# One decoder step with a routed mixture of experts: expert products on four 32-column strips, turned by VectorE

## The chip, the cores and the metric

The kernel runs on one core of a Trainium2 chip. The metric is device time in microseconds (us), lower is better; a time is the median of several executions of the whole program. One program computes the whole step; the change touches its expert phase and the layouts of what that phase reads.

## The reference

One layer of a decoder over 2048 prompt tokens and 32 sample tokens (2080 in all), 1024 wide, in fp32. After attention and a recurrent branch comes the part that matters here:

```python
def hier_moe(x, ...):            # top-1 group of 4, then top-2 of the 8 experts in it
    gates = p_sel * softmax(top_val)            # two (token, expert) pairs per token: 4160 pairs
    return routed_experts(x, experts.reshape(-1), gates.reshape(-1), w1, w3, w2)

def expert_block(args):          # rows of one expert; w1, w3: 1024 x 512, w2: 512 x 1024, 32 experts
    xb = x_pad[toks]
    hb = silu(xb @ w1[e]) * (xb @ w3[e])
    return hb @ w2[e]
# the results, times their gates, are summed per token; then x + gate2 * ffn and a final RMSNorm
```

## The kernel before

The phases follow one another: modulation and input projection, attention for both groups, the router (with the output projection), the experts, the final sum. Each phase has one hand-written stream for each engine, ordered by semaphores only.

The router writes each token's row twice (once for each chosen expert) into DRAM scratch: `xs_d0` holds the left 512 columns, `xs_d1` the right 512, rows grouped by expert. It also counts, for each expert, how many blocks of G = 64 rows it has. `experts_of` then loops over the 32 experts, and inside over the blocks of an expert (a hardware loop with a count read from memory). On this data there are 80 blocks: 1 to 4 for an expert, 2.5 on average. `n` counts blocks over all experts.

One block, engine by engine:

- GpSimd (`gpsimd`): `load(n)` waits until TensorE has turned the block before, then brings 64 rows with two DMAs (`xs_d0` to partitions 0 to 63 of `x_in`, `xs_d1` to 64 to 127; there is one such buffer). `store(n)` waits until the copy two blocks back is in `y` and until the store before has landed, then writes 64 rows of `ys_d` with one DMA. Its DRAM side is `strips`: "r (s n) -> s r n" with two strips of 512 columns, so the outermost dimension is 2. Both use GpSimd's own DMA queue (q0).
- TensorE (`tensor`): in a block, `hidden` makes x @ [w1 | w3] in two halves of 128 hidden columns on two strips (64 tokens stand as 64 columns of the array, the output lands in partitions 0 to 63 or 64 to 127): 8 chunks of 128 inputs, 2 strips, 2 halves, 256 columns each, 32 products. `turn_hidden` turns a half of the gated values through the array (L1982), `turn(n + 1)` turns the next block's rows (4 transposes, L1968), `out` makes the product with w2: 8 products of 512 columns (L1989). In the trace each fp32 product is two matmul instructions, each with its own weight load; a transpose is one.
- ScalarE (`scalar`): two sigmoids, and the copy of the turned rows from PSUM to `xT` (L1952).
- VectorE (`vector`): two multiplications for each half, the copy of the turned values to `hT` (L2027), the copy of the result to `y` (L2035).
- SyncE (`sync`): the weights, three slots. Expert e's w1, w3 and w2 (2 MB each) are issued when the last block of expert e - 3 is done (`hold` on `y`). The DRAM side is "(c p) n -> p c n": in a partition, 8 rows of 2 KB of w1 that lie 128 rows apart. They use q1.

Two buffers of `y` let results run one block ahead of their stores. What sets the order around the change: the program order of each engine, the semaphores above, and the order of DMAs inside each of the two queues.

Of the kernel before, what the change touches and what calls it, by code (L numbers as in the profile page):

```python
# [35 lines left out]
STRIPS = 2  # L36
G = P // STRIPS
XW = D // STRIPS
# [31 lines left out]
class Kit:  # L70
# [768 lines left out]
def attention_phase(nc, io, keep, sems):  # L839
# [38 lines left out]
    with ExitStack() as stack:  # L878
        k = Kit(nc, stack)
        shared = keep["w13_0"][:, :, :, :].rearrange("p c a n -> p (c a n)")  # L880
# [535 lines left out]
def router(nc, io, keep, sems, k):  # L1416
# [59 lines left out]
    def sync(sp):  # L1476
# [19 lines left out]
        for at, name in enumerate(("w1", "w3")):  # L1496
            sp.dma_start(keep["w13_0"][:, :, at, :], io[name][0, 0].rearrange("(c p) n -> p c n", p=P)).then_inc(sems["pre"], 16)
# [11 lines left out]
    def gpsimd(pool):  # L1509
# [31 lines left out]
        pool.dma_start(io["ys_d"][0:G, :].rearrange("r (s n) -> s r n", n=XW), keep["y"][:, 0, :]).then_inc(sems["st"], 16)  # L1541
# [301 lines left out]
def experts_of(nc, io, keep, sems, k, emptied):  # L1843
# [8 lines left out]
    x_in, xT = keep["o_rs"][:, :, :].rearrange("p c n -> p (c n)"), keep["o_sq"]  # L1852
    sg, hid = k.sb("sg7", [P, 2, P]), k.sb("hid", [P, 2, P])
    hT = k.sb("hT", [P, 2, P])
    y = keep["y"]
    xb, yb = keep["banks"][5], keep["banks"][3]
    h, tb = ([keep["banks"][b] for b in pair] for pair in ((4, 6), (0, 1)))
    s = {n: k.sem(f"p7_{n}") for n in ("in", "xT", "xe", "h", "sg", "hid", "hT", "he", "y", "ye", "sp")}
# [3 lines left out]
    ident = keep["ident"]  # L1862
    src = {n: io[n][0] for n in ("w1", "w3", "w2")}
    def strips(d, row):

        return d[ds(row, G), :].rearrange("r (s n) -> s r n", n=XW)

# [16 lines left out]
    def sync(sp):  # L1884
# [3 lines left out]
        sp.dma_start(w2[0][:, :, :], src["w2"][0].rearrange("(c p) n -> p c n", p=P)).then_inc(s_w2[0], 16)  # L1888
        sp.wait_ge(sems["placed"], 1)
        sp.wait_ge(s["in"], 32)  # L1890
        for e in range(NE):
# [27 lines left out]
    def gpsimd(pool):  # L1919
        pool.nop().then_inc(s["ye"], 2)  # L1920
        pool.nop().then_inc(s["xT"], 1)
# [23 lines left out]
        hold(pool, s["st"], 16 * n + 48, s["sp"])  # L1945
        hold(pool, s["in"], 32 * n + 32, s["sp"])

    def scalar(act):
        def turned(n):

            act.wait_ge(s["xT"], n + 2)
            act.activation(xT[:, :, :], xb[:, :].rearrange("p (c n) -> p c n", n=P), ACT.Copy).then_inc(s["xe"], 1)  # L1952

        def body(n, e, b, extra):
            for half in range(2):
                act.wait_ge(s["h"], 2 * n + half + 1)
                act.activation(sg[:, half, :], h[half][:, 0:P], ACT.Sigmoid).then_inc(s["sg"], 1)  # L1957
            turned(n + 1)

        act.wait_ge(sems["placed"], 1)  # L1960
        turned(0)
        experts(act, body)

    def tensor(pe):
        def turn(n):
            pe.wait_ge(s["in"], 32 * n + 32)
            for c in range(XW // P):
                mm = pe.transpose(xb[:, c * P:c * P + P], x_in[:, c * P:c * P + P], ident[:, :])  # L1968
            mm.then_inc(s["xT"], 1)

        def hidden(i, half, chunks):

            for c in chunks:
                for q in range(STRIPS):
                    cols = slice(q * (DE // STRIPS) + half * P, q * (DE // STRIPS) + half * P + P)
                    mm = pe.matmul(h[half][q * G:q * G + G, 0:2 * P], xT[:, c % (XW // P), c // (XW // P) * G:c // (XW // P) * G + G],  # L1976
                                   w13[i][:, c, :, cols], start=(c == 0), stop=(c == KC - 1))
            return mm

        def turn_hidden(n, half):  # L1980
            pe.wait_ge(s["hid"], 2 * n + half + 1)
            pe.transpose(tb[half][:, 0:P], hid[:, half, :], ident[:, :]).then_inc(s["hT"], 1)  # L1982

        def out(i, n, half):

            pe.wait_ge(s["he"], 2 * n + half + 1)
            for q in range(STRIPS):
                for p in range(STRIPS):
                    mm = pe.matmul(yb[p * G:p * G + G, :], hT[:, half, q * G:q * G + G], w2[i][:, q * (EC // STRIPS) + half, p * XW:p * XW + XW],  # L1989
# [293 lines left out]
```

## Time and profile before

| | |
|---|---|
| median of 3 executions | 2929.57 us (2927.0 to 2935.26) |
| span of the profiled execution | 2942.9 us, 13.3 us above that median; no other time of that execution is shown |
| instructions | 45551 |
| TensorE busy | 2701.4 us, 92% of the span |
| weight loads | 1377.9 us (47%), beside the matmuls |
| VectorE, ScalarE, GpSimd busy | 46%, 33%, 16% |
| DMA | 575.74 MB, mean 196 GB/s |
| expert phase | 1852.4 to 2844.0 us of the span, 991.6 us |

Busy is the time in which an engine had at least one instruction in flight. Weight loads are counted apart, as PEld. The name of a tile is the program's first name for that memory: in the expert phase `o_rs` is the landing buffer of the rows, `o_sq` the turned rows, `w`, `oT` and `w_out` the three weight slots.

### The profile page before, as it was taken

Reading aid. Unit: us, or ns where it says so; the run is one execution under the profiler, and the core shown is the slowest. Engines: PE = TensorE matmul, PEld = TensorE weight load, DVE = VectorE, ACT = ScalarE, POOL = GpSimd, SP = SyncE. Lnnn points to the kernel's source line nnn. Section 1 sums busy time; section 2 is a strip of 40 time slices with the busy share of each in tenths; the row PEclk is TensorE's granted clock in tenths of the full one; section 3 lists DMA queues with packets and bytes.
Section 4 is the critical chain, followed back from the end, with each engine's and each line's share of the span. In section 5 each row is a group of like instructions: output and inputs, shape, how many; then the busy total and the mean of one; then the engine's idle time right before and its main releaser. Section 6 shows DMA issues by size and latency. Waiting matters only on the chain. (4 is left out here: it accounts for less than half of the span.)

```text
span 2942.9 us, 45551 instructions
## 1 busy us (share of the span) xinstructions
PE 2701.4 (92%) x15113; PEld 1377.9 (47%) x15113; DVE 1352.6 (46%) x2734; ACT 961.6 (33%) x1858; POOL 472.9 (16%) x669
## 2 busy tenths in 40 slices
PE   6999999976988898998989997799999998899978
PEld 3444444433544444554535554355545554455533
DVE  2241414143887787897867776122112221122118
ACT  2222222113777776787842221100000010000004
POOL 0101010101112111211201223111111111111123
PEclk8999999997999999999999998899999999999989
DMA  8020201146667776767763334686976679969637
GB/s 321 15 86 15 81 19 65 50 148 223 212 224 261 227 242 214 250 211 245 234 231 114 129 129 157 217 280 216 300 236 216 212 234 357 305 215 300 215 103 318
DMA packets 275921, 575.74 MB, mean 196 GB/s; under 512 B 59270, under 2 KB 75719, under 8 KB 271740
## 3 DMA queue, kind: packets, MB, share of 16 engines
q1 hardware_dynamic: 192936, 427.99, 42.1%
q0 software_dynamic: 82480, 145.43, 15.4%
q8 instruction: 89, 1.46, 0.2%
q14 instruction: 92, 0.75, 0.1%
q10 hardware_dynamic: 324, 0.10, 0.0%
HBM read 460.86 MB, written 112.29 MB: 195 GB/s over the span
## 5 line engine op out<-in xcount | busy, mean ns | idle before, releaser
L1246 DVE TENSOR_TENSOR_SCAN left<-leave,left 128x512 f32<-128x512 f32 (+3 forms) x320 | 358.6, 1121 | 138.6 <-ACT leave L1128 137.9
L435 PE MATMUL bank<-xnT,w_in 128*128 128x512 f32 x768 | 330.3, 592 | 0.0
L1989 PE MATMUL bank<-w,hT 128*64 128x512 f32 x1280 | 315.1, 614 | 0.0
L1957 ACT ACTIVATE sg<-bank 128x128 f32<-128x128 f32 x160 | 44.3, 277 | 688.0 <-PE bank L1976 688.0
L1049 POOL DMA_DIRECT2D w_out<-in_cache_v x256 | 137.4, 537 | 666.8 <-issue 663.9
L1976 PE MATMUL bank<-w,o_sq 128*64 128x256 f32 x1920 | 224.2, 387 | 9.5 <-DMA w<-in_w 6.7
L435 PEld LDWEIGHTS bank<-xnT,w_in 128*128 128x128 f32 x768 | 145.6, 190 | 181.8 <-issue 179.4
L1612 PE MATMUL bank<-w_out,w 128*128 128x512 f32 x512 | 227.7, 597 | 2.6 <-DVE w L1676 2.6
L435 PE MATMUL bank<-w_in,xnT 128*128 128x512 f32 x512 | 220.4, 592 | 0.0
L2021 DVE TENSOR_TENSOR sg<-sg,bank 128x128 f32<-128x128 f32 x160 | 46.1, 288 | 375.3 <-ACT sg L1957 375.3
L1976 PE MATMUL bank<-oT,o_sq 128*64 128x256 f32 x1856 | 212.3, 381 | 0.3 <-issue 0.3
L1297 PE MATMUL tb<-ident,take 128*128 128x128 f32 x1088 | 182.5, 285 | 29.6 <-DVE take L1152 25.9
L1128 ACT ACTIVATE leave<-zb,nbiasP 128x512 f32<-128x512 f32 (+3 forms) x320 | 204.3, 638 | 8.1 <-PE zb L1290 8.0
L1130 ACT ACTIVATE take<-zb,biasP 128x512 f32<-128x512 f32 (+3 forms) x320 | 206.9, 647 | 0.0
L1152 DVE TENSOR_TENSOR take<-take,left 128x512 f32<-128x512 f32 (+3 forms) x320 | 194.8, 609 | 15.5 <-DVE left L1246 0.5
L1284 PE MATMUL zb<-w 64*128 64x512 f32 (+3 forms) x640 | 165.5, 595 | 30.4 <-ACT take L1130 19.1
L1297 PEld LDWEIGHTS tb<-ident,take 128*128 128x128 f32 x1088 | 120.5, 143 | 148.1 <-issue 80.2
L1332 PE MATMUL tb<-ident,w_out 128*128 128x128 f32 x1024 | 161.5, 282 | 25.2 <-DMA w_out<-in_cache_k 15.8
L1976 PEld LDWEIGHTS bank<-w,o_sq 128*64 128x64 f32 x1920 | 137.6, 139 | 95.5 <-issue 32.0
L1060 ACT ACTIVATE wT<-tb 128x512 f32<-128x512 f32 (+3 forms) x240 | 131.8, 549 | 126.8 <-PE tb L1297 126.1
L1976 PEld LDWEIGHTS bank<-oT,o_sq 128*64 128x64 f32 x1856 | 131.3, 137 | 80.8 <-issue 18.8
L1932 POOL DMA_DIRECT2D ys_d<-y x82 | 70.3, 857 | 551.5 <-DMA ys_d<-y 437.5
(411 smaller groups left out, 3386.5 us busy)
## 6 DMA issues: line engine op xcount, KB each, us to landing
w<-in_w SPq DMA_DIRECT2D x54, 2048.0 KB, 23.6
w_out<-in_cache_v POOLq DMA_DIRECT2D x256, 256.0 KB, 5.1
w_out<-in_cache_k SPq DMA_DIRECT2D x256, 256.0 KB, 4.0
oT<-in_w SPq DMA_DIRECT2D x22, 2048.0 KB, 19.5
w_out<-in_w SPq DMA_DIRECT2D x20, 2048.0 KB, 18.7
ys_d<-zeros SPq DMA_DIRECT2D x32, 816.0 KB
ys_d<-y POOLq DMA_DIRECT2D x83, 256.0 KB, 10.3
o_rs<-xs_d POOLq DMA_DIRECT2D x162, 128.0 KB, 6.4
```

Of the source, the lines that this page charges most:

```text
L435: mm = pe.matmul(ps[:, :], w, m, start=(i == 0), stop=(i == len(parts) - 1))
L1049: pool.dma_start(vp[g % 2][:, j, :], cache["cache_v"][ds(number, 1)].rearrange("a p n -> (a p) n")).then_inc(s_vp[g % 2], 16)
L1128: act.activation(leave[n % 4][:, 0:cols], zb[n % 3][:, 0:cols], ACT.Sigmoid, scale=-SCALE, bias=keep["nbiasP"][:, head:head + 1]).then_inc ...
L1130: act.activation(take[n % 4][:, 0:cols], zb[n % 3][:, 0:cols], ACT.Sigmoid, scale=SCALE, bias=keep["biasP"][:, head:head + 1]).then_inc(s_ ...
L1152: dve.tensor_tensor(take[n % 4][:, 0:cols], take[n % 4][:, 0:cols], left[n % 4][:, 1:cols + 1], ALU.mult).then_inc(s_w, 1)
L1246: dve.tensor_tensor_scan(left[n % 4][:, 0:cols][:, ::-1], leave[n % 4][:, 0:cols][:, ::-1], leave[n % 4][:, 0:cols][:, ::-1], left[n % 4][ ...
L1284: mm = pe.matmul(zb[(n + par) % 3][:, 0:cols], qT[pair % 2][half, t * P:t * P + P], kT[pair % 2][half, c * GRP:c * GRP + cols], start=True ...
L1297: mm = pe.transpose(to[:, j * P:j * P + P], take[n % 4][:, j * P:j * P + P], ident[:, :])
L1332: mm = pe.transpose(to[:, i * P:i * P + P], kp[g % 2][:, i, f * P:f * P + P], ident[:, :])
L1612: mm = pe.matmul(pb[half][0:n, :], lhs, w_out[:, half, c, :], start=(c == 0), stop=(c == KC - 1))
L1976: mm = pe.matmul(h[half][q * G:q * G + G, 0:2 * P], xT[:, c % (XW // P), c // (XW // P) * G:c // (XW // P) * G + G], w13[i][:, c, :, cols] ...
L1989: mm = pe.matmul(yb[p * G:p * G + G, :], hT[:, half, q * G:q * G + G], w2[i][:, q * (EC // STRIPS) + half, p * XW:p * XW + XW], start=(hal ...
```

## The change

The block stays 64 rows, but the array is now used in 4 strips of Q = 32 columns: one block is 2 units of 32 tokens (UNITS), and the four strips of a unit are four ranges of 128 hidden columns (or of 256 output columns). `hidden(i, u)` is 8 chunks times 4 strips, 256 columns each; `out(i, u)` is 4 chunks times 4 strips, 256 columns each: 96 products for a block where there were 40.

All transposes through TensorE go. VectorE's `transpose`, which turns 32x32 squares inside their place, turns the rows (`turn_rows`, 128x256 for each unit) and the gated values (128x128 for each unit). For this the squares must find their weight rows in matching order: the weights are loaded as "(p c) n -> p c n", so that a partition holds 8 rows of w1 that follow one another in DRAM, 16 KB in one piece on both sides (`w13` becomes [P, 2, KC, DE] for that), and 4 rows of w2 likewise, 16 KB. ScalarE copies the landed rows into the order that the squares want (`landed`), and takes over the copy of the result from PSUM.

The rows land in two buffers (in `rowsP`). A load of a block is 4 DMAs of 64 partitions x 1 KB, a store 2 DMAs of 128 partitions x 1 KB. Both have `in_strips` as their DRAM side: "b (s n) -> s b n"; a load's strips there are 2, a store's 4. `load` now ends with a wait for its own landing, ahead of `store`. w1 and w3 of a slot are released after the first product of its last block, w2 after the second, and TensorE waits for w2 only ahead of `out`.

```diff
-STRIPS = 2
-G = P // STRIPS
-XW = D // STRIPS
+G = 64
+STRIPS = 4
+Q = P // STRIPS
+UNITS = G // Q
+XW = UNITS * (D // STRIPS)
...
+def in_strips(d, row, u):
+    return d[ds(row + u * Q, Q), :].rearrange("b (s n) -> s b n", n=D // STRIPS)
...
-                hold(sp, s["y"], sp.snap(done, min_val=1, max_val=MAX_BLOCKS), s["sp"])
+                freed = sp.snap(done, min_val=1, max_val=MAX_BLOCKS)
+                hold(sp, s["h1"], freed, s["sp"])
...
-                    sp.dma_start(w13[i][:, :, at, :], src[name][e].rearrange("(c p) n -> p c n", p=P)).then_inc(s_w13[i], 16)
+                    sp.dma_start(w13[i][:, at, :, :], src[name][e].rearrange("(p c) n -> p c n", p=P)).then_inc(s_w13[i], 16)
...
+            if e >= SLOTS:
+                hold(sp, s["y"], freed, s["sp"])
             if e > 0:
-                sp.dma_start(w2[i][:, :, :], src["w2"][e].rearrange("(c p) n -> p c n", p=P)).then_inc(s_w2[i], 16)
+                sp.dma_start(w2[i][:, :, :], src["w2"][e].rearrange("(p j) n -> p j n", p=P)).then_inc(s_w2[i], 16)
...
         def load(n, row):
-            hold(pool, s["xT"], n + 1, s["sp"])
-            for half in range(2):
-                pool.dma_start(x_in[64 * half:64 * half + 64, :], strips(io[f"xs_d{half}"], row)).then_inc(s["in"], 16)
+            hold(pool, s["cp"], n + 1, s["sp"])
+            for u in range(UNITS):
+                for half in range(2):
+                    pool.dma_start(x_in[64 * half:64 * half + 64, ds(n & 1, 1), u * (XW // 2):(u + 1) * (XW // 2)].rearrange("p a n -> p (a n)"),
+                                   in_strips(io[f"xs_d{half}"], row, u)).then_inc(s["in"], 16)
+            hold(pool, s["in"], 64 * n + 64, s["sp"])
...
-            hold(pool, s["st"], 16 * n + 16, s["sp"])
-            pool.dma_start(strips(io["ys_d"], n * G + G), y[:, ds(n & 1, 1), :].rearrange("p a n -> p (a n)")).then_inc(s["st"], 16)
+            hold(pool, s["st"], 32 * n + 32, s["sp"])
+            for u in range(UNITS):
+                pool.dma_start(in_strips(io["ys_d"], n * G + G, u),
+                               y[:, ds(n & 1, 1), u * (XW // 2):(u + 1) * (XW // 2)].rearrange("p a n -> p (a n)")).then_inc(s["st"], 16)
...
+        def landed(n):
+            act.wait_ge(s["in"], 64 * n + 64)
+            act.wait_ge(s["xT"], 2 * n + 1)
+            act.activation(x_turn[:, :].rearrange("p (u c a) -> p u c a", u=UNITS, c=KC),
+                           x_in[:, ds(n & 1, 1), :].rearrange("p z (u a c) -> p (z u) c a", u=UNITS, c=KC), ACT.Copy).then_inc(s["cp"], 1)
...
+        def result(n):
+            act.wait_ge(s["st"], 32 * n + 64)
+            act.wait_ge(s["y"], n + 1)
+            act.activation(y[:, ds(n & 1, 1), :].rearrange("p a n -> p (a n)"), yb[:, :], ACT.Copy).then_inc(s["ye"], 1)
         def body(n, e, b, extra):
+            landed(n + 1)
+            for u in range(UNITS):
+                gated(n, u)
+            result(n)
...
+        def hidden(i, u):
+            for c in range(KC):
                 for q in range(STRIPS):
+                    mm = pe.matmul(h[u][q * Q:q * Q + Q, 0:2 * P], xT[:, c, u, :], w13[i][:, :, c, q * P:q * P + P], start=(c == 0), stop=(c == KC - 1))
...
+        def out(i, u):
+            for j in range(EC):
+                for q in range(STRIPS):
+                    mm = pe.matmul(yb[q * Q:q * Q + Q, u * (XW // 2):(u + 1) * (XW // 2)], hT[:, u, j, :], w2[i][:, j, q * (XW // 2):(q + 1) * (XW // 2)],
+                                   start=(j == 0), stop=(j == EC - 1))
...
         def body(n, e, b, extra):
             i = e % SLOTS
+            for u in range(UNITS):
+                pe.wait_ge(s["xT"], 2 * n + u + 2)
+                hidden(i, u).then_inc(s[f"h{u}"], 1)
+            pe.wait_ge(s_w2[i], 16 * (e // SLOTS) + 16)
+            for u in range(UNITS):
+                pe.wait_ge(s["hT"], 2 * n + u + 1)
+                mm = out(i, u)
+            mm.then_inc(s["y"], 1)
...
+        def turn_rows(n, u):
+            dve.wait_ge(s["cp"], n + 3)
+            dve.transpose(xT[:, :, u, :], x_turn[:, u * (XW // 2):(u + 1) * (XW // 2)]).then_inc(s["xT"], 1)
         def body(n, e, b, extra):
+            for u in range(UNITS):
+                dve.wait_ge(s["sg"], 2 * n + u + 1)
+                dve.tensor_tensor(sg[:, u, :], sg[:, u, :], h[u][:, 0:P], ALU.mult)
+                dve.drain()
+                dve.tensor_tensor(hid[:, u, :], sg[:, u, :], h[u][:, P:2 * P], ALU.mult)
+                dve.drain()
+                dve.transpose(hT[:, u, :, :].rearrange("p j b -> p (j b)"), hid[:, u, :].rearrange("p (a j) -> p j a", j=EC)).then_inc(s["hT"], 1)
+                turn_rows(n + 1, u)
```

## Rows read from the trace of the kernel before

**Rows 1.** Engine busy time in stretches: us, (x instructions), clock, DMA share, GB/s
```profile
2287.10:2333.50 46.40, 46.40 (x346) 24.93 (x344) 9.72 (x28) 4.61 (x12) 7.60 (x13) 1.00 0.55 181
2453.50:2468.50 15.00, 12.21 (x89) 6.24 (x85) 3.12 (x8) 1.15 (x3) 1.92 (x3) 0.98 1.05 360
1852.40:2844.00 991.60, 950.35 (x6880) 504.62 (x6880) 193.58 (x559) 97.22 (x244) 153.57 (x240) 0.98 0.75 249
```

**Rows 2.** Timeline of TensorE, one block: start, us, line, shapes, x instructions
```profile
2298.70 5.78 PE L1976 MATMUL bank<-oT,o_sq 128*64 128x256 f32 x52
2304.41 0.33 PE L1982 MATMUL bank<-ident,hid 128*128 128x128 f32 x1
2308.00 0.60 PE L1968 MATMUL bank<-ident,o_rs 128*128 128x128 f32 x4
2308.54 1.94 PE L1989 MATMUL bank<-w,hT 128*64 128x512 f32 x8
2310.31 1.90 PE L1976 MATMUL bank<-oT,o_sq 128*64 128x256 f32 x16
```

**Rows 3.** Timeline of TensorE elsewhere: products on four strips of 32 columns
```profile
674.44 1.04 PE L727 MATMUL ps_mod<-ig,cT 128*32 128x512 f32 x8
675.30 1.04 PE L727 MATMUL ps_mod<-yb,cT 128*32 128x512 f32 x8
753.86 0.88 PE L1368 MATMUL tb<-kT_new,q_blk 128*32 128x4 f32 x32
```

**Rows 4.** Groups of instructions in the expert phase: busy, mean ns | idle before, releaser
```profile
L2035 DVE COPY y<-bank 128x512 f32 x79 | 54.7, 692 | 221.0 <-PE bank L1989 195.9 <-DMA ys_d<-y 25.1
L1982 PE MATMUL bank<-ident,hid 128*128 128x128 f32 x160 | 52.5, 328 | 0.0
L1952 ACT ACTIVATE o_sq<-bank 128x512 f32<-128x512 f32 x80 | 47.8, 597 | 204.8 <-PE bank L1968 204.8
L2027 DVE COPY hT<-bank 128x128 f32<-128x128 f32 x160 | 46.7, 292 | 196.3 <-PE bank L1982 196.3
L2021 DVE TENSOR_TENSOR sg<-sg,bank 128x128 f32<-128x128 f32 x160 | 46.1, 288 | 375.3 <-ACT sg L1957 375.3
```

**Rows 5.** Timeline of ScalarE and VectorE behind the last product of a second half
```profile
1954.13 1.89 PE L1989 MATMUL bank<-w,hT 128*64 128x512 f32 x8
1954.34 0.28 ACT L1957 ACTIVATE sg<-bank 128x128 f32<-128x128 f32 x1 [3.59 <-PE bank L1976]
1955.02 0.29 DVE L2023 TENSOR_TENSOR hid<-sg,bank 128x128 f32<-128x128 f32 x1
```

**Rows 6.** Timeline of GpSimd's DMA issues
```profile
1965.34 0.86 POOL L1932 DMA_DIRECT2D ys_d<-y  x1 [6.63 <-DMA ys_d<-y]
1975.84 0.86 POOL L1932 DMA_DIRECT2D ys_d<-y  x1 [5.54 <-DMA ys_d<-y]
2309.41 1.06 POOL L1926 DMA_DIRECT2D o_rs<-xs_d  x2 [5.00 <-PE bank L1968]
```

**Rows 7.** Who waited for whom in the expert phase: us, times, longest
```profile
POOL ys_d L1932 <- DMA ys_d<-y: 437.5, 64, 12.3
PE bank L1968 <- DMA o_rs<-xs_d: 29.5, 16, 4.0
```

**Rows 8.** DMA from 2209 to 2219 us, one store and two loads, little else
```profile
GB/s 0 0 0 0 0 0 0 36 4 37 19 33 16 0 0 0 33 33 0 49 49 49 66 33 66 66 33 66 33 66 66 33 66 33 66 279 229 246 147 246
DMA packets 631, 0.55 MB, mean 55 GB/s; under 512 B 493, under 2 KB 493, under 8 KB 631
q0 software_dynamic: 621, 0.53, 21.5%
ys_d<-y POOLq DMA_DIRECT2D x1, 256.0 KB, 9.0
o_rs<-xs_d POOLq DMA_DIRECT2D x2, 128.0 KB, 2.5
```

**Rows 9.** DMA from 1975.8 to 1981.6 us, a store beside the weights
```profile
DMA packets 1228, 2.11 MB, mean 364 GB/s; under 512 B 208, under 2 KB 208, under 8 KB 1227
q1 hardware_dynamic: 1027, 2.07, 100.7%
ys_d<-y POOLq DMA_DIRECT2D x1, 256.0 KB, 13.5
```

**Rows 10.** DMA from 1486 to 1495 us: rows of 16 KB into rowsP
```profile
DMA packets 169, 1.67 MB, mean 186 GB/s; under 512 B 24, under 2 KB 24, under 8 KB 73
```

More of the change, by code:

```diff
@@ L1851, in experts_of @@
     w13, w2 = [keep[f"w13_{i}"] for i in range(SLOTS)], [keep[f"w2_{i}"] for i in range(SLOTS)]
[L1852 to L1854 removed]
+    x_in = keep["rowsP"][:, 2, :].rearrange("p (a n) -> p a n", a=2)
+    x_turn = keep["o_rs"][:, :, :].rearrange("p c n -> p (c n)")
+    xT = keep["o_sq"][:, :, :].rearrange("p c n -> p (c n)").rearrange("p (c u b) -> p c u b", c=KC, u=UNITS)
+    sg, hid = k.sb("sg7", [P, UNITS, P]), k.sb("hid", [P, UNITS, P])
+    hT = k.sb("hT", [P, UNITS, EC, Q])
     y = keep["y"]
[L1856 to L1858 removed]
+    yb, h = keep["banks"][3], [keep["banks"][b] for b in (4, 6)]
+    s = {n: k.sem(f"p7_{n}") for n in ("in", "cp", "xT", "h0", "h1", "sg", "hT", "y", "ye", "sp")}
     s["st"] = sems["st"]
@@ L1944, in gpsimd @@
         store(n + 1)
-        hold(pool, s["st"], 16 * n + 48, s["sp"])
-        hold(pool, s["in"], 32 * n + 32, s["sp"])
+        hold(pool, s["st"], 32 * n + 96, s["sp"])
     def scalar(act):
-        def turned(n):
-            act.wait_ge(s["xT"], n + 2)
-            act.activation(xT[:, :, :], xb[:, :].rearrange("p (c n) -> p c n", n=P), ACT.Copy).then_inc(s["xe"], 1)
-        def body(n, e, b, extra):
[L1955 to L1958, printed above, removed]
+        def landed(n):
[3 more added lines that the diff above has]
+                           x_in[:, ds(n & 1, 1), :].rearrange("p z (u a c) -> p (z u) c a", u=UNITS, c=KC), ACT.Copy).then_inc(s["cp"], 1)
@@ new lines, in gated @@
+        def gated(n, u):
+            act.wait_ge(s[f"h{u}"], n + 1)
+            act.activation(sg[:, u, :], h[u][:, 0:P], ACT.Sigmoid).then_inc(s["sg"], 1)
+        def result(n):
+            act.wait_ge(s["st"], 32 * n + 64)
+            act.wait_ge(s["y"], n + 1)
+            act.activation(y[:, ds(n & 1, 1), :].rearrange("p a n -> p (a n)"), yb[:, :], ACT.Copy).then_inc(s["ye"], 1)
+        def body(n, e, b, extra):
+            landed(n + 1)
+            for u in range(UNITS):
+                gated(n, u)
+            result(n)
@@ L1960, in scalar @@
+        act.nop().then_inc(s["xT"], 1)
         act.wait_ge(sems["placed"], 1)
-        turned(0)
+        landed(0)
         experts(act, body)
     def tensor(pe):
[L1965 to L1973, printed above, removed]
+        def hidden(i, u):
+            for c in range(KC):
@@ L1984, in out @@
[L1984 to L1989, printed above, removed]
-                                   start=(half == 0 and q == 0), stop=(half == 1 and q == STRIPS - 1))
+                    mm = pe.matmul(h[u][q * Q:q * Q + Q, 0:2 * P], xT[:, c, u, :], w13[i][:, :, c, q * P:q * P + P], start=(c == 0), stop=(c == KC - 1))
@@ L1994, in body @@
             i = e % SLOTS
-            pe.wait_ge(s["xe"], n + 1)
-            hidden(i, 0, range(KC)).then_inc(s["h"], 1)
-            hidden(i, 1, range(5))
-            turn_hidden(n, 0)
-            hidden(i, 1, range(5, KC)).then_inc(s["h"], 1)
-            out(i, n, 0)
-            turn_hidden(n, 1)
-            turn(n + 1)
-            out(i, n, 1).then_inc(s["y"], 1)
+            for u in range(UNITS):
[6 more added lines that the diff above has]
+            mm.then_inc(s["y"], 1)
         def before(e):
@@ L2010, in before @@
                 pe.wait_ge(s_w13[i], 32 * (e // SLOTS + (1 if i else 0)))
[L2011 removed]
         pe.wait_ge(sems["placed"], 1)
[L2014 removed]
         experts(pe, body, before)
     def vector(dve):
+        def turn_rows(n, u):
+            dve.wait_ge(s["cp"], n + 3)
+            dve.transpose(xT[:, :, u, :], x_turn[:, u * (XW // 2):(u + 1) * (XW // 2)]).then_inc(s["xT"], 1)
         def body(n, e, b, extra):
[L2019 to L2021 removed]
+            for u in range(UNITS):
+                dve.wait_ge(s["sg"], 2 * n + u + 1)
+                dve.tensor_tensor(sg[:, u, :], sg[:, u, :], h[u][:, 0:P], ALU.mult)
                 dve.drain()
[L2023 to L2036 removed]
+                dve.tensor_tensor(hid[:, u, :], sg[:, u, :], h[u][:, P:2 * P], ALU.mult)
+                dve.drain()
+                dve.transpose(hT[:, u, :, :].rearrange("p j b -> p (j b)"), hid[:, u, :].rearrange("p (a j) -> p j a", j=EC)).then_inc(s["hT"], 1)
+                turn_rows(n + 1, u)
+        for u in range(UNITS):
+            turn_rows(0, u)
         experts(dve, body)
```

46 lines of the change are left out of this document (10 added, 36 removed).

## The prediction

> **What bounds the kernel now.** I read the stretches of the expert phase first, as nothing else in the program changes its work. The phase lasts 991.6 us, TensorE is busy in 950.35 of them at clock 0.98 [rows 1]. Then one block on TensorE's timeline: from one block's first product (2298.70) to the next one's (2310.31) are 11.61 us, with no idle time in an expert of four blocks (46.40 busy of 46.40) [rows 1, 2]. The 80 blocks (160 L1982, two for each block [rows 4]) at 11.61 would take 929 us, so 63 us go elsewhere: experts of one block, which wait for 6.3 MB of weights (15.0 us for one block, DMA share 1.05 [rows 1]), the first expert, and 29.5 us in which TensorE waits for rows [rows 7]. So TensorE bounds it, but something stands close behind: GpSimd's stores wait 437.5 us in all for the store before to land [rows 7]. Stores issued at 1965.34 and 1975.84 are 10.5 us apart, with 5.54 us of waiting on the landing [rows 6]. A chain of transfers with a period of 10.5 to 14 us (9.0 to 13.5 for the landing [rows 8, 9]) lies under a product chain of 11.6 us. The reader is to see both before pricing a faster TensorE.
>
> **Products: 96 for 40.** The new block has 64 + 32 products, 192 matmul instructions of 256 columns. On four strips the trace has 512 columns: 8 instructions start at 674.44 and the next 8 at 675.30, 0.43 us for four abreast [rows 3]. Half the columns: 0.215 us for four, 48 x 0.215 = 10.3 us for a block. The same columns on two strips also make 10.3 (64 instructions of 256 columns and 16 of 512, two abreast), so the strips bring nothing by themselves. That 32-column instructions can follow one another fast enough is seen where they have 4 columns: 32 in 0.88 us, 0.028 each, against the 0.054 wanted [rows 3]. What goes is the rest, 11.61 - 10.3 = 1.3 us a block: two turns of gated values, four of rows, and the changes of shape around them [rows 2]. 80 x 1.3 = 104 us if nothing else binds.
>
> The Trainium skill (TensorE: Matmul & The Clock Gate, "The mechanism" of packing) says that a weight load overlaps products in flight only when they stand in different row groups, and here all four strips share all rows; by that, 192 loads would queue up. At 0.11 us or more each that page's rule would put over 20 us on a block; the eight instructions in 0.86 us say otherwise.
>
> **The turned values.** In the old trace the sigmoid of the second half starts 0.21 us after the next product's start (1954.34 against 1954.13), and its second multiplication ends at 1955.31, 1.18 us after it [rows 5]. A VectorE transpose isn't in the trace. Nearest is the copy of the same 128x128 shape, 0.29 us; the 128x512 copy at 0.69 is the upper bound, and below 0.29 would gain nothing because TensorE is busy [rows 4]. With 0.29 and 0.1 for the handover they are there at 1.6 us; the first unit's `out` (32 instructions at 0.054) covers 1.7. So nothing, at most 0.3 x 80 = 24 us.
>
> **ScalarE and VectorE.** ScalarE gets two 128x512 copies (0.60 each by the nearest [rows 4], up to double for the strided read) and two sigmoids of 0.28 [rows 5]: 1.8 to 3 us of 10.3. VectorE: four multiplications, two 128x128 and two 128x256 transposes, 2.6 to 4.5 us. Both wait in program order, but `landed(n + 1)` stands ahead of the sigmoids: rows that land late hold up the block in hand, once the two buffers are used up. All of this hides unless the rows are late, and that is the question.
>
> **The transfers.** A store now is 256 KB in two strips. In a quiet stretch a store and two loads (0.53 MB) leave 621 packets, 493 of them below 512 B, and through most of it only 33 to 66 GB/s flow [rows 8]. With the weights 16 engines move 364 GB/s, 23 each [rows 9]: the store flows over two engines. 0.53 MB in the 128 other packets is 4 KB each, so 64 for the store, 32 for each of two engines, and 14 x 32 = 448 of the small ones are the fillers of the other 14. It lands after 9.0 us in quiet and after 13.5 beside the weights [rows 8, 9]: 4.5 / 32 = 0.14 us for each place in the queue, about one weight packet (1027 packets of 2.07 MB, 2 KB each, 0.09 us at 23 GB/s; w2's are 4 KB, 0.18). So the two queues take turns packet by packet on each engine, fillers too.
>
> The Trainium skill (DMA: Bandwidth & Descriptors, "Queues, rings and completion order") gives the rule that the engines used are the largest number up to 16 that divides the outermost dimensions of both sides; the store's two agree with it.
>
> The new load's DRAM side has two strips outermost: two engines for each of its four DMAs, 64 KB / 2 / 4 KB = 8 places. The store's two DMAs have four strips: 128 KB / 4 / 4 KB = 8 places. Together 6 x 8 = 48 places on every engine for a block, against 32 + 2 x 2 = 36 now. And the weights become rows of 16 KB in one piece. The one transfer of such rows in the trace has 169 packets for 1.67 MB, 96 of them of 8 KB or more: they go as 16 KB packets [rows 10]. At 23 to 26 GB/s that is 0.63 to 0.7 us, four to seven times what a place costs now beside the weights.
>
> The loop on GpSimd, free of weights: four issues, 3 x 0.53 and then the landing, 2.5 [rows 6, 8], 4.1; register work between a landing and the store's issue 0.9 (1975.84 less 1965.34 less about 9.5); two stores at 0.6 to 0.86, 1.5; back to the next load 1.1 (0.8 from the release to the issue: 2308.60 to 2309.41 [rows 2, 6]). 7.6 us, well under 10.3. But `load` waits for its landing before `store` and before the next load, so the loop can't run ahead while weights stream. An expert has 6.3 MB / 16 KB / 16 = 24 weight packets on each engine, 15.6 us at 0.65. In that time at most 24 places are served, half a block: a load caught in it stands until the weights are in. What the loop still does in it is issuing, 3.6 us. So it loses 12 us for each expert. Bounds: 8 (a whole loop's own work falls into the stream) to 15.6.
>
> Sum, for an expert of 2.5 blocks: 2.5 x 7.6 + 12 = 31 us, plus 0.8: the four experts of one block take 15 us by the weights alone [rows 1], 7 over a loop. 31.8, x 32 = 1018 us, against 991.6. TensorE alone would need 2.5 x 10.3 = 25.8. The gain of 104 us is hidden behind the transfers, and 26 us are added: the span goes from 2942.9 to 2969. Its execution stood 13.3 above the median; at the median, 2929.6 + 26 = 2955. With 8 and 15.6 for 12: 890 and 1133 us, 2830 and 3070.
>
> **Rivals.** *TensorE keeps the pace.* If loads spread over 16 engines (their SBUF side has 64 partitions outermost), or weights stay in small packets, or 16 KB packets don't make the small ones wait, the loop stays under 10.3: 80 x 10.3 = 825, plus the 15 us of the first expert and 10 to 20 for experts of one block, 850 to 860, which is 2790 to 2800, and 2820 with the upper bound of the turned values; I take 2800. For it: a load that finds the queue empty lands in 2.5 us; against it: the fillers. *Half and half:* late rows only in experts of one or two blocks, 2850 to 2915. *The strips don't run abreast at 256 columns* (slower): if a group of four takes 0.43 us whatever its columns, a block takes 20.6 us and the phase 1650, over 3500; if weight loads cost 0.02 us an instruction, 14 us, 3070 and more. It decides once four instructions need over 0.24 us; the 0.028 us [rows 3] speaks against it. *The change doesn't do what it says:* weight rows that aren't joined to 16 KB give the first rival.
>
> **Numbers.** Transfers set the pace (own range 2925 to 3040): 0.50, of it 0.45 slower and 0.05 no change. TensorE keeps the pace: 0.33, faster. Half and half: 0.12, of it 0.09 faster and 0.03 no change. Strips: 0.05, slower. Faster 0.42, no change 0.08, slower 0.50; no change is within 0.3%, about what this kernel's timing can tell. The range from 2790 to 3020 leaves out some of the first rival below, and the strips and the worst transfers above.
>
> **What would show it.** Four products start within 0.03 us and the next four 0.215 later; blocks in quiet stretches take 10.3 to 10.6 us; weight packets of 16 KB, 384 for an expert; loads with fillers of their own, so more packets below 512 B than now; loads that land after over 10 us beside weights; TensorE and ScalarE waiting for the landing of rows, 150 us or more in all. Wrong would be: loads landing in 3 to 5 us throughout, or a phase below 900 us.

## The result, and the profile after

The changed kernel takes 3141.1 us (median of 6 runs, 3131.1 to 3163.3), the one before 2934.2 us beside it (6 runs): a ratio of 1.0725, 95% interval 1.0701 to 1.0750. Slower, as forecast, but by 207 us where 26 were forecast, and above the range's 3020 us.

The stretches of the profiled execution (start:end, length, busy time of TensorE's products and weight loads, VectorE, ScalarE, GpSimd, then clock, DMA share, GB/s): the expert phase, and two blocks in it that met no delay.

```profile
1846.50:3058.20 1211.70, 895.97 (x15358) 498.39 (x15360) 206.49 (x641) 184.41 (x327) 326.29 (x482) 0.87 0.60 204
2656.00:2679.00 23.00, 23.00 (x428) 13.13 (x424) 5.29 (x16) 5.24 (x9) 8.13 (x12) 0.99 0.56 174
```

The phase is 220 us longer than the 991.6 of [rows 1]; the rest of the program is 7 us shorter. TensorE has less work in it (896 us for 950) and stands idle for 316. Its timeline in the second stretch (start, us, line, x instructions):

```profile
2657.05 7.08 PE L1993 MATMUL bank<-w,o_sq 128*32 128x256 f32 x128
2663.95 3.70 PE L2000 MATMUL bank<-w,hT 128*32 128x256 f32 x64
2667.47 7.09 PE L1993 MATMUL bank<-w,o_sq 128*32 128x256 f32 x128
```

From one block's first product to the next one's are 10.42 us, against 11.61 in [rows 2] and 10.3 in the forecast. That part of the change does what it says. The groups of the phase (busy, mean ns of one, idle before, releaser), against [rows 4]:

```profile
L1935 POOL DMA_DIRECT2D rowsP<-xs_d x317 | 210.4, 672 | 81.6 <-issue 80.7 <-ACT o_rs L1965 0.6
L1965 ACT ACTIVATE o_rs<-rowsP 128x512 f32 x80 | 91.7, 1147 | 455.7 <-DMA rowsP<-xs_d 454.2 <-issue 1.3
L2037 DVE STREAM_TRANSPOSE hT<-hid 128x128 f32<-128x128 f32 x160 | 66.2, 414 | 12.6 <-issue 0.6
L2028 DVE STREAM_TRANSPOSE o_sq<-o_rs 128x256 f32<-128x256 f32 x160 | 64.4, 402 | 0.0
L1975 ACT ACTIVATE y<-bank 128x512 f32 x80 | 47.8, 597 | 387.2 <-PE bank L2000 337.4 <-DMA ys_d<-y 49.8
```

And who waited for whom (us, times, longest), against [rows 7]:

```profile
POOL ys_d L1944 <- issue: 735.2, 85, 34.1
ACT o_rs L1965 <- DMA rowsP<-xs_d: 454.2, 65, 28.0
PE bank L2000 <- DVE hT L2037: 315.2, 38, 33.4
```

The three waits are one. GpSimd stands at `load`'s wait for the landing before it may issue the store, ScalarE waits for the same rows, and TensorE for the values behind ScalarE. The timeline of all engines shows it once:

```profile
2071.73 2.65 POOL L1935 DMA_DIRECT2D rowsP<-xs_d  x4 [0.52 <-issue]
2075.01 7.09 PE L1993 MATMUL bank<-w_out,o_sq 128*32 128x256 f32 x128
2094.86 1.12 ACT L1965 ACTIVATE o_rs<-rowsP 128x512 f32 x1 [18.78 <-DMA rowsP<-xs_d]
2095.66 1.41 POOL L1944 DMA_DIRECT2D ys_d<-y  x2 [21.28 <-issue]
2096.18 0.29 DVE L2033 TENSOR_TENSOR sg<-sg,bank 128x128 f32<-128x128 f32 x1 [23.01 <-ACT sg L1970]
2097.36 1.94 PE L2000 MATMUL bank<-w,hT 128*32 128x256 f32 x16 [15.26 <-DVE hT L2037]
```

Rows issued from 2071.7 on have all landed at 2094.6. TensorE ends the block's first products at 2082.1 and waits 15.26 us: `landed(n + 1)` stands ahead of the sigmoids of block n, so rows that are late for the next block hold the one in hand. The DMA packets from 2076 to 2094 us say what was in the way (weights are q1, rows q0):

```profile
DMA packets 1003, 5.78 MB, mean 321 GB/s; under 512 B 590, under 2 KB 590, under 8 KB 671
q1 hardware_dynamic: 379, 5.42, 80.8%
q0 software_dynamic: 623, 0.34, 8.2%
```

332 packets (1003 less 671) are of 8 KB or more and 5.42 MB / 332 are 16 KB each: the weights come in packets of 16 KB. The rows' 623 packets need only 8.2% of the engines' time; most of the 23 us they aren't being moved, and the likeliest reading is that they stand in line behind the others; experiments 1 and 11 test it. The forecast had this picture and this price. What it hadn't is the other kind of block, free of weights; GpSimd's timeline of two:

```profile
2258.50 1.41 POOL L1944 DMA_DIRECT2D ys_d<-y  x2 [21.19 <-issue]
2260.43 2.65 POOL L1935 DMA_DIRECT2D rowsP<-xs_d  x4 [0.52 <-issue]
2268.28 1.41 POOL L1944 DMA_DIRECT2D ys_d<-y  x2 [5.20 <-issue]
2270.20 2.65 POOL L1935 DMA_DIRECT2D rowsP<-xs_d  x4 [0.52 <-issue]
2277.92 1.41 POOL L1944 DMA_DIRECT2D ys_d<-y  x2 [5.07 <-issue]
2280.96 2.66 POOL L1935 DMA_DIRECT2D rowsP<-xs_d  x4 [1.62 <-issue]
```

9.8 and 10.8 us from load to load, of which 5.1 to 5.2 pass between the end of the load's issues and the store. I split the loops by the trace's packets, each loop counted from the landing of one block's rows to the landing of the next: in 36 of 78 weight packets take under 0.3 us of an engine's time between the last issue of the load and its landing. These take 10.27 us on average, with 1.98 from the first issue to the last and 4.3 from there to the landing. The other 42 take 18.7, and land after 13.1. So 80 x 10.27 = 822, and the other 390 us of the phase are 12.6 for each of the 31 experts whose weights stream. That is a remainder. By the loops themselves 42 x 8.45 = 355 us are lost, 11.4 for an expert; most of what is left is the first block, ahead of whose second product TensorE waits longest, 33.4 us (the longest wait in the list above). Forecast were 7.6 for the free loop and 12 for the loss. The loss was right in size; the free loop was not.

### The profile page after: what moved, and what is told of

Its sections match the earlier page's. It is cut to its first block and busy times, and to the rows that moved or that the text cites. A ratio compares the mean times of both kernels' runs of the same rounds, so it can differ in the third digit from the quotient of the medians.

```text
span 3155.8 us, 63798 instructions
## 1 busy us (share of the span) xinstructions
PE 2642.2 (84%) x23589; PEld 1368.9 (43%) x23589; DVE 1365.3 (43%) x2816; ACT 1051.0 (33%) x1942; POOL 647.3 (21%) x914
## 5 line engine op out<-in xcount | busy, mean ns | idle before, releaser
L2000 PE MATMUL bank<-w,hT 128*32 128x256 f32 x5120 | 348.2, 431 | 315.2 <-DVE hT L2037 315.2
L2000 PEld LDWEIGHTS bank<-w,hT 128*32 128x32 f32 x5120 | 173.0, 124 | 483.3 <-DVE hT L2037 347.9
L1944 POOL DMA_DIRECT2D ys_d<-y x164 | 115.9, 712 | 810.0 <-issue 743.6
L1965 ACT ACTIVATE o_rs<-rowsP 128x512 f32 (+1 forms) x81 | 92.9, 1146 | 464.6 <-DMA rowsP<-xs_d 454.2
L1935 POOL DMA_DIRECT2D rowsP<-xs_d x324 | 215.1, 672 | 85.1 <-issue 84.2
L1993 PE MATMUL bank<-w,o_sq 128*32 128x256 f32 x3840 | 214.7, 382 | 20.0 <-DVE o_sq L2028 20.0
L1993 PE MATMUL bank<-oT,o_sq 128*32 128x256 f32 x3712 | 205.6, 379 | 0.5 <-issue 0.5
L1975 ACT ACTIVATE y<-bank 128x512 f32 x80 | 47.8, 597 | 387.2 <-PE bank L2000 337.4
## 6 DMA issues: line engine op xcount, KB each, us to landing
w<-in_w SPq DMA_DIRECT2D x54, 2048.0 KB, 15.9
```

Of the source, the lines that this page charges most:

```text
L1935: pool.dma_start(x_in[64 * half:64 * half + 64, ds(n & 1, 1), u * (XW // 2):(u + 1) * (XW // 2)].rearrange("p a n -> p (a n)"), in_strips( ...
L1993: mm = pe.matmul(h[u][q * Q:q * Q + Q, 0:2 * P], xT[:, c, u, :], w13[i][:, :, c, q * P:q * P + P], start=(c == 0), stop=(c == KC - 1))
L2000: mm = pe.matmul(yb[q * Q:q * Q + Q, u * (XW // 2):(u + 1) * (XW // 2)], hT[:, u, j, :], w2[i][:, j, q * (XW // 2):(q + 1) * (XW // 2)], s ...
```

## The experiments

All were timed beside the kernel before, whose median was between 2931 and 2937 us. "Phase" is the expert phase of the profiled execution; free loop, landing and loss are worked out as above, the loss with that run's own free loop. The changed kernel's profiled execution took 3157 us, 16 above its median, so what is saved against its phase of 1211.7 comes out about 16 us larger than in the medians.

**1. Weights in small packets.** The order of the pieces in SBUF gives 2 KB for w1 and w3, four DMAs 4 KB for w2.

```
-  w13_0 [P, 2, KC, DE];  w13[i][:, at, :, :]
+  w13_0 [P, KC, 2, DE];  w13[i][:, :, at, :]
-  sp.dma_start(w2[i][:, :, :], ...)
+  for j in range(EC): sp.dma_start(w2[i][:, j, :], ...[:, j, :])
```

> The changed kernel, but w1 and w3 land as [c, a, n] in SBUF, so that their pieces are 2 KB instead of 16 KB, and w2 comes in four DMAs of 4 KB rows; the order of the rows is the same. Theory A (GpSimd's loop of loads and stores sets the pace, and what it loses beside the weights is a 16 KB packet for each place in the queue): a place costs 0.09 to 0.18 us beside weights instead of 0.65, so of the 12.6 us lost for an expert some 5 remain; phase 80 x 10.27 + 31 x 5 = 980 us instead of 1212, time about 2910. The landing of rows beside weights falls from 13 to about 9 us. Theory B (only the loop's serial waits and issues matter, not the packet size): within 1% of 3141. Theory C (weights get slower with small packets, 16.5 us of engine time for an expert against 15.6): slightly above 3141.

Measured: 3050.8 us, ratio 1.0404 (1.0346 to 1.0461). Phase 1102. The free loop stays (10.34), the loss falls to 8.9. The direction is A's, with 90 us well short of the 231 it gave. The landing beside weights falls from 13.1 to 9.6 us, as A has it, but now 55 of 78 loads meet weights where 42 did, and the other term isn't touched.

**2. Loads on 16 engines.** Each of the four loads of a block brings one strip for all 64 rows, so that 32 pairs of rows stand outermost on the DRAM side.

```
-  for u in range(UNITS):
-      for half in range(2):
-          pool.dma_start(x_in[64 * half:64 * half + 64, ...], in_strips(io[f"xs_d{half}"], row, u))
+  for q in range(STRIPS):
+      pool.dma_start(x_in[q * Q:q * Q + Q, ...], one_strip(io[f"xs_d{q // 2}"], row, q % 2))
...
+  one_strip: d[ds(row, G), strip s].rearrange("(u b) n -> b u n", u=UNITS)
```

> The changed kernel, but each of the four load DMAs takes one strip of all 64 rows, so that 32 rows stand outermost on both sides and all 16 DMA engines share it: 1 place in the queue on each engine instead of 8, 20 places for a block instead of 48. Stores and weights as they are. Theory A: fillers and places matter. Free of weights the last load lands about 2.5 us after its issue instead of 4.3, the loop takes 8.5; beside weights a load waits behind the store's 16 places at 0.65, 10.4 us, so some 9 are still lost for an expert; phase about 2.6 x 8.5 x 31 + 9 x 31 = 960, TensorE's 10.4 a block just below; time about 2890. Theory B (serial waits, not places): the free landing stays near 4.3, time within 1% of 3141.

Measured: 3025.4 us, 1.0317 (1.0248 to 1.0385). Phase 1081. Both terms fall: the free loop to 9.44 (8.8 median), with the landing 2.4 us after the last issue for 4.3, and the loss to 10.5, with the landing beside weights at 10.5 us for 13.1. The median falls by 116 us, of A's 250. The DMA view of 8 us with one quiet load and a store, first of the changed kernel (from 2270), then of this one (from 2904.7):

```profile
DMA packets 767, 0.52 MB, mean 65 GB/s; under 512 B 643, under 2 KB 643, under 8 KB 767
rowsP<-xs_d POOLq DMA_DIRECT2D x4, 64.0 KB, 3.4
```

```profile
DMA packets 302, 0.50 MB, mean 63 GB/s; under 512 B 180, under 2 KB 180, under 8 KB 302
rowsP<-xs_d POOLq DMA_DIRECT2D x4, 64.0 KB, 3.0
```

The same bytes with 463 fewer small packets (the four loads' 4 x 14 x 8 = 448 fillers). The medians differ by 0.4 us only, because a median over four hides the last: in the quiet loops of the changed kernel the first three loads land on average 2.9 to 3.1 us after their own issue and the fourth after 4.3, here all four after 2.4 to 3.1, and the fourth is the one GpSimd waits for.

**3. The wait moved.** GpSimd issues the store before it waits for the load's landing.

```
   load(n, ...)   # without its hold
   store(n)
+  hold(pool, s["in"], 64 * n + 64, s["sp"])
```

> The changed kernel, but the wait for the rows' landing stands behind the store instead of ahead of it. Every load still lands before the next is issued. Theory A: the free loop is then issues and one landing side by side with the stores: 4 x 0.67 + 2 x 0.7 + register work 1.5 + what is left of the landing, 8 us instead of 10.27, below TensorE's 10.4, but the 12.6 us lost beside weights stay, since the next load still waits: 31 x (2.6 x 8 + 12.6) = 1035, time about 2965. Theory B (the serial wait is the whole cause): TensorE's pace, 2810. Theory C (DMA places alone, the order of waits is nothing): 3141.

Measured: 3079.1 us, 1.0500 (1.0438 to 1.0562). Phase 1136. Between A and C, nowhere near B: the landing itself is still in the loop of rows, only the store's issue isn't behind it any more. The terms behave as A has them: the free loop falls, though to 9.4 and not to 8, and the loss stays (12.4).

**4. 16 KB packets alone, in the kernel before.** Its products read the weights as they come, so the values are not the reference's.

```
-  src[name][e].rearrange("(c p) n -> p c n", p=P)
+  src[name][e].rearrange("(p c) n -> p c n", p=P)     # and w13 [P, 2, KC, DE], w2 likewise
```

> The kernel before, with one part of the change alone: weights come as 16 KB rows. The products then pair the wrong inputs with weight rows, so the output isn't the reference's; the work is the same. Theory A: a store has 32 places on each engine, an expert's weights 24 packets, so a store beside weights lands after 9 + 24 x 0.65 = 24 us instead of 13.5. The chain of stores, 10.4 us free, gets 12 to 15 us more for an expert: phase 32 x (2.5 x 10.4 + 13) = 1250, time about 3190, slower than before by 8 to 9%. Theory B (packet size doesn't matter, or larger is better): within 1% of 2934.

Measured: 3094.6 us, 1.0553 (1.0487 to 1.0619). One part of the change by itself costs 158 us. Its waits, against [rows 7]:

```profile
POOL ys_d L1932 <- DMA ys_d<-y: 506.7, 56, 26.5
PE bank L1968 <- DMA o_rs<-xs_d: 175.5, 33, 20.1
```

TensorE waits 175.5 us for rows where it waited 29.5, once for 20.1 us. The old load, on few and small packets, suffers from 16 KB neighbours as well. The weights themselves come sooner: the page of the profile has 19.9 us to landing for 2 MB into the first slot in place of 23.6.

**5. Loads and stores on 16 engines.** As 2, and the store in four strips too.

> The changed kernel with every transfer of rows cut by strips of 64 rows: four loads and four stores for a block, each of which lands on 16 engines with one place; the weights still come in packets of 16 KB. It differs from the run that cut the loads alone (3025 us) by the store: two transfers of two engines have become four of sixteen. Theory A (GpSimd's chain sets the pace; packets behind weight packets of 16 KB are what a place costs): the store's 16 places and its small packets on idle engines go, but GpSimd issues two more transfers, 2 x 0.7 us a block. Beside weights the first saves about 3 us per expert, the issues cost up to 1.4 x 80 = 112 us where nothing hides them and nothing where GpSimd waits for the landing anyway: 3000 us (2970 to 3050). Theory B (the number of issues on GpSimd is what sets the free loop): 3025 + 112 = 3137 us. Theory C (the store's small packets are what slows the loads): 2930 us.

Measured: 2997.7 us, 1.0216 (1.0189 to 1.0243). Phase 1060. A. (The store it replaces has four strips outermost in each of its two transfers, so four engines each and not two.) Two more issues a block don't cost 112 us (B): the free loop is 9.8 for 9.4. And the store's small packets aren't what held the loads (C). With 48, 20 and now 8 places for a block on an engine, rows beside weights land after 13.1, 10.5 and 8.5 us, and the loss is 12.6, 10.5 and 8.9: fewer places help, but far from in proportion.

**6. Both cuts.** 1 and 2 together.

> The changed kernel with two of its parts undone together: each load one strip of 64 rows on 16 engines, and the weights in packets of 2 and 4 KB. Alone they took the expert phase from 1211.7 us to 1081 and to 1102. Theory A (a chain on GpSimd with a free loop and a loss per expert, which the two cut in different places): free loop 9.44 us as with the loads alone, x 80 = 755; loss per expert 12.6 in the changed kernel, 10.5 with the loads cut, 3.4 less with small packets: 7.1 x 31 = 220; phase 975 us, which is 236 less than the changed kernel's: 2905 us (2870 to 2940). Theory B (TensorE at its own pace of 10.42 us a block is already the bound once one of them is gone): 80 x 10.42 + the 63 us that the kernel before also lost = 897 us, 2827 us. Theory C (both remove the same delay, small packets queued behind packets of 16 KB): no better than the loads alone, 3000 to 3025 us.

Measured: 2896.3 us, 0.9875 (0.9847 to 0.9902), faster than before. Phase 946 (A: 975). 110 + 131 = 241 us were the two alone, 266 together (in the medians 90 + 116 = 206, and 245 together). Neither takes away what the other brings, so they aren't one delay seen twice (C). Together they bring 25 to 40 us more than the sum; with two runs for each of the two alone that is hardly beyond the noise, and no run says where it comes from.

**7. Both cuts and the wait.** 1, 2 and 3 together.

> As the run before it, and GpSimd's wait for the landing of the load stands behind the issue of the store. Alone that took the phase of the changed kernel from 1211.7 to 1136 us. Theory A (what is left of the landing on GpSimd's chain goes; half of those 75 us were beside packets of 16 KB, which are gone here): 2905 - 35 = 2870 us, at or a little above TensorE's pace. Theory B (TensorE bounds both): the same time as the run before it within 0.3%, both near 2827 us. Theory C (the wait is independent of the rest): 2905 - 75 = 2830 us, with the run before at 2905.

Measured: 2823.7 us, 0.9609 (0.9579 to 0.9640), the fastest. Its phase and one of its waits:

```profile
1845.90:2725.10 879.20, 846.98 (x15360) 492.34 (x15360) 210.84 (x641) 188.97 (x327) 287.21 (x480) 0.98 0.85 281
```

```profile
ACT o_rs L1972 <- DMA rowsP<-xs_d: 143.6, 55, 7.2
```

TensorE is busy in 847 of 879 us; 80 blocks at 10.42 are 834. The gain over the kernel before is 112 us of phase, against the 104 that the forecast counted and then hid. This lies on C's number and within 50 us of A's; B is wrong, as the run before it isn't at TensorE's pace, though this one nearly is.

**8. And the store on 16 engines.** 7, with 5's store.

> As the run before it, and the store in four transfers of 16 engines. Theory A (GpSimd is by now close to free, the store's landing is hidden): the two added issues of 0.7 us cost nothing or up to 30 us: 2870 to 2900 us. Theory B (TensorE bounds): the same as the run before it. Theory C (the store's landing on two engines with its small packets still held the chain): 30 to 50 us faster than the run before it, 2830 us.

Measured: 2823.7 us, 0.9626 (0.9600 to 0.9651). The same as 7 (B): with TensorE as the bound the store doesn't matter.

**9. Half of the first product.** Is the free loop GpSimd's own, or TensorE's 10.42 us in disguise? They are nearly equal. The values are not the reference's.

```
-  for c in range(KC):
+  for c in range(KC // 2):
```

> The changed kernel with half of the first product left out (its inner loop runs over 4 of the 8 pieces, so the values are not the reference's): TensorE needs about 3.7 + 3.5 = 7.2 us for a block in place of 10.42. All transfers stay. The question is whether the 10.27 us of a block free of weights are GpSimd's own chain or TensorE's pace. Theory A (the chain of transfers alone): block and phase stay, 3141 us (3125 to 3150). Theory B (free blocks run at TensorE's pace, and what GpSimd would gain in them was never there): they fall to the 7.6 us of the forecast, 36 x 2.65 = 95 us less, and blocks beside weights gain up to 1 us: 3000 to 3045 us.

Measured: 3160.3 us, 1.0789 (1.0751 to 1.0827).

```profile
1849.50:3064.00 1214.50, 647.90 (x10239) 344.58 (x10240) 200.96 (x641) 177.93 (x327) 326.01 (x482) 0.78 0.60 203
```

TensorE loses 248 us of work and the phase keeps its length: 1214.5 for 1211.7. The free loop is 10.21, the landing 4.33. So it is A: the products don't set the length of the phase. The total stands 10 us over the upper end of what A was given; the two profiled executions are 3.7 us apart, and where the rest is from stays open. The granted clock of the phase is 0.78 where it was 0.87, with less work for TensorE, so the lower clock isn't what makes the changed kernel slow either.

**10. The same with loads on 16 engines.**

> The same half of the products left out in the kernel whose loads land on 16 engines (3025 us; free block 9.44 us on average, 8.8 median). Theory A (its free block is GpSimd's chain too: issues 2.0, landing 2.2 to 2.4, and 3.9 around them, 8.4 us): 3025 - 32 x 1.0 = 2990 us. Theory B (TensorE's pace of 10.42 us held it back, and each block after a delay beside weights could catch up): free block at 8.0 us or less and 2 us less beside weights, 2900 to 2950 us. Theory C (nothing but the weights' delay counts): 3025 us.

Measured: 3035.7 us, 1.0364 (1.0325 to 1.0402), no faster than 2, which had twice the first product. That is C's number. The free loop has fallen to 8.9 as A has it, but the loss rose from 10.5 to 12.3 (33 loops beside weights of 19.7 us), and the phase is 1093 for 1081: a faster TensorE gives no more time to a chain that waits for weights to pass. Against 9, from which only the loads differ, the free loop falls by 1.3 us and the phase by 122 (1214.5 to 1092.7); 80 x 1.3 are 104 of them. B's 50 us and more of catching up don't exist.

**11. No weights.** From expert 3 on one row of one piece stands in for each weight transfer; the values are not the reference's.

```
-  sp.dma_start(w13[i][:, at, :, :], src[name][e]...)
+  sp.dma_start(w13[i][0:1, at, 0:1, :], src[name][e]...[0:1, 0:1, :])      # e >= SLOTS; w2 likewise
```

> The changed kernel in which the weights of experts 3 and above are left out (one row of one piece stands in for each transfer, so the values are not the reference's); products, loads and stores of rows stay. Theory A (a loss of 12.6 us per expert beside weights, on top of a free block of 10.27 us): 80 x 10.27 + 35 us for the first experts, which still load theirs = 857 us in place of 1211.7, so 2787 us, with GpSimd's loads landing 4.3 us after the last issue in nearly all blocks. Theory B (with the weights gone the landing falls to the 2.5 us that the forecast took, and TensorE's pace of 10.42 us bounds): about the same time, 2790 us, but landing 2.5 us and GpSimd waiting for the products. Theory C (part of the loss comes from handing over between experts, not from the weights): 2880 us or more.

Measured: 2825.5 us, 0.9646 (0.9610 to 0.9682). Phase, waits and the page's DMA issues:

```profile
1845.80:2725.40 879.60, 839.79 (x15360) 491.77 (x15360) 211.41 (x641) 193.77 (x327) 325.48 (x482) 0.98 0.29 74
```

```profile
ACT sg L1971 <- PE bank L1994: 319.0, 151, 3.2
POOL ys_d L1945 <- ACT y L1976: 244.8, 46, 5.9
```

```profile
ys_d<-y POOLq DMA_DIRECT2D x166, 128.0 KB, 3.7
rowsP<-xs_d POOLq DMA_DIRECT2D x324, 64.0 KB, 3.3
```

332 us of the 1211.7 are the weights' doing (316 in the medians). The last load still lands 4.41 us after its issue (75 loops), so that time isn't the weights': here B is wrong. But A's 857 is 22 short, since at 10.42 us TensorE is now the slower of two nearly equal chains (10.40 a loop), which is B's half of the truth; and the first block, beside weights of the first experts that still come, takes 47 us from its first product to the next block's:

```profile
1845.82 9.26 PE L1994 MATMUL bank<-w,o_sq 128*32 128x256 f32 x128 [20.04 <-DVE o_sq L2029]
1888.46 4.98 PE L2001 MATMUL bank<-w,hT 128*32 128x256 f32 x64 [33.37 <-DVE hT L2038]
1893.26 7.08 PE L1994 MATMUL bank<-w,o_sq 128*32 128x256 f32 x128
```

**12. Small packets and the wait, loads as changed.**

> The changed kernel with weights in packets of 2 and 4 KB (alone 3051 us) and GpSimd's wait for the landing moved behind the store (alone 3079 us), the loads as changed, on two engines each. Theory A (independent terms): 3141 - 90 - 62 = 2989 us. Theory B (both are needed for TensorE to keep its pace; each alone leaves a delay that the other would remove): 2900 to 2940 us, at least 30 us below the sum. Theory C (the loads on two engines with 8 places keep the landing above a block's time beside weights whatever GpSimd waits for): 3030 us.

Measured: 2965.9 us, 1.0125 (1.0075 to 1.0175). Phase 1025: 1211.7 - 110 - 75 = 1027, so the two are independent as far as the noise lets one see (A, though the total is 23 us under A's). Without the loads on 16 engines it isn't enough: this kernel is still slower than before.

## Why the prediction was wrong, point by point

- **What bounds the kernel now; two chains, one close under the other.** Right. Experiment 9 shows that in the changed kernel the products aren't the bound, and 1, 2, 3 and 11, each of which changes the chain of transfers and takes 62 to 316 us away, that this chain is.
- **Products.** 10.3 us a block forecast, 10.42 measured, in spite of weight loads in one row group. The rule of the Trainium skill (TensorE: Matmul & The Clock Gate, "The mechanism") that loads overlap only across row groups isn't borne out here: 192 instructions on strips of 32 columns start in 10.42 us, 0.054 each, while weight loads are busy in 13.13 of 23.00 us beside a TensorE that is busy in all 23.00. Four start within 0.01 us and the next four 0.216 later (2657.047 to 2657.057, then 2657.263).
- **Turned values, ScalarE and VectorE.** The transpose took 0.41 us where 0.29 was assumed and 0.69 the bound, the strided copy of landed rows 1.15 for "0.60 up to double". Blocks of 10.42 us show both hidden.
- **Transfers beside the weights.** 16 KB packets, two engines, fillers: all as written. The loss of 12 us per expert measured 12.6 as a remainder, 11.4 by the loops. Part luck is in this: the picture was one load for each expert that stands until the weights are in, and measured are 42 delayed loops for 31 experts that lose 8.45 us each. The rule on the engines used, which the prediction puts under another heading, stands in the Trainium skill (DMA: Bandwidth & Descriptors) in "Why a DMA increments its semaphore by 16 and not by 1"; experiment 2 agrees with it, as the fillers of the loads go when 32 pairs of rows stand outermost. What brings the loss down is shown apart: small packets bring 110 us of phase (1), 16 engines 131 (2), and the 16 KB packets alone cost the old kernel 158 us (4).
- **The loop on GpSimd, free of weights, 7.6 us. This is the step that failed:** it takes 10.27. Of the 2.7 us, 2.2 are in its first term, "3 x 0.53 and then the landing, 2.5, 4.1", which measures 1.98 + 4.31 = 6.3; the remaining 3.5 us of register work and stores are 4.0. The issues take 0.67 each in place of 0.53; in experiment 2 they take 0.54 again, but the first and the last still start 2.0 us apart. The 2.5 was a row of the *old* load [rows 8], two DMAs of 2 places on all engines; the same paragraph counts four of 8 places for the new one, up to 32 on an engine. The store in the same rows, 32 places and 9.0 us to landing, spoke against 2.5. The trace's packets show both: the 64 packets of 4 KB of the old load start within 1.3 us (2217.65 to 2218.93), 1.1 to 2.4 us after its issue at 2216.53; of the quiet new one that GpSimd issues from 2260.43 to 2262.41 the last six start 0.155 us apart, as one engine would do them one after the other (each takes 0.159), and the last at 2266.54. Eight pieces in a row in place of two are 6 x 0.155 = 0.9 of the 1.8 us that the landing is longer. The other half isn't explained. It can't be that all four loads share two engines, as from 2264.8 to 2265.6 four packets of 4 KB run side by side; and only the fourth load is so late (experiment 2). The number was read off a form that the change removes. Loads on 16 engines bring the landing to 2.4 and the loop to 8.9 where products don't hold it (10).
- **The sum.** With the measured loop and the forecast's own other numbers: 2.5 x 10.27 + 12 + 0.8 = 38.5 us an expert, x 32 = 1231, against 1211.7 measured. The miss is 1211.7 - 1018 = 194 us of phase (186 in the medians, 3141 less 2955); the 2.5 x 2.67 x 32 = 213 us of the free loop are more than all of it. Experiments 9 and 10 show the term at work: 1.3 us less of free loop, 122 us less of phase. The sum stands on 80 free loops and was far more sensitive to them than to the loss per expert, for which alone it had bounds (8 and 15.6). There the range went wrong: no bound was given to 7.6.
- **Rivals.** "TensorE keeps the pace", 2800 us, is what experiments 7 and 11 reach (2824 and 2825) once loads go over 16 engines, weights come in small packets and a wait moves that it didn't name, or once the weights are gone. It had its conditions joined by "or": one of them alone left 3025 or 3051 us, and the two together 2896. "The strips don't run abreast" is refuted by the products above.
- **What would show it.** Loads landing over 10 us beside weights, waits for rows over 150 us: seen. "Blocks in quiet stretches take 10.3 to 10.6": in quiet stretches TensorE does run at 10.4, but GpSimd at 10.3 just under it, so a block lost beside weights was never made up. Loads landing in 3 to 5 us, a sign of being wrong had it been so throughout, were seen in the 36 quiet loops.

The version with 16-engine loads, small weight packets and the moved wait is faster than both kernels: 2824 us, 0.961 of the kernel before.

## What to carry to other kernels

Price a transfer by the row whose form it will have (engines used, pieces on each), not by the row of the tensor that it brings: here the old load said 2.5 us, the store, on two engines as the new loads are, said 9, and the new loads took 4.3. When a shorter product chain is put over a chain of transfers, count that chain's quiet period as carefully as its worst one, and bound it, since it is multiplied by every block. One 16 KB weight packet is cheap for itself and dear for whoever takes turns with it.

## What the runs showed of the hardware beyond this

- VectorE's transpose in 32x32 squares took 414 ns for 128x128 and 402 ns for 128x256 values: the larger no longer than the smaller. The smaller reads its values regrouped (`(a j) -> j a`), the larger in order; no run takes the two apart.
- ScalarE's copy within SBUF with a regrouped read of 128x512 values took 1147 ns, the plain one out of PSUM 597.
- Weights of 2 MB into the first slot landed in 15.9 us (changed), 19.9 (before, 16 KB) and 23.6 (before), medians: larger packets help the weights while they hurt the rows, 149 us of phase in experiment 4.
- GpSimd's issue of one load took 0.67 us when two strips stood outermost and 0.54 when 32 did, yet four of them took 2.0 us from the first start to the last in both.
- Of four loads of 64 KB in a quiet loop the fourth landed 4.3 us after its issue on two engines, the first three 2.9 to 3.1; with loads and stores on 16 engines (experiment 5) all four took 2.2.
- TensorE's granted clock over the phase was 0.98 with 840 of 880 us busy, 0.87 with 896 of 1212 and 0.78 with 648 of 1215; in the last two the phase was equally long.
